# Output projection under the last page's steps, triangular inversion by 64x64 chunks, and the order of the router's last tile, in a hybrid decoder step

## The chip, the cores and the metric

The kernel runs on one core of a Trainium2 chip. The metric is the device time of one execution in microseconds, the median of the runs.

## The reference

One decoder layer for a prompt of 256 tokens and 8 sampled tokens, width 1024, float32, one set of weights for both:

- `p = RMSNorm(h) @ w_in`; its columns feed a gated DeltaNet (4 heads of 128) and a latent attention (4 heads).
- DeltaNet, prompt: exact chunked form, chunk 64. In each chunk and head `lower = tril(k_b k^T * decay, -1)`, `wy = inverse(eye + lower)`, `u = wy @ v_b`, `w = wy @ (k_b exp(g))`, then a scan over the 4 chunks. Sampled tokens: one step of the recurrence on a state of 128x128 a head and token; norm and gate on both.
- Latent attention, sampled tokens: scores against 2048 cached latents each (8 sequences, read through a page table), softmax, sum of latents; prompt: causal.
- `h = h + concat(DeltaNet, latent attention) @ w_out`, where the first 512 rows of `w_out` belong to DeltaNet and the last 512 to the latent attention.
- `h = h + CrossAttention(RMSNorm(h), K and V of RMSNorm(memory))`, then `h = h + MoE(RMSNorm(h))`, top 4 of 32 experts, and a final RMSNorm.

## The kernel before, in words

Every engine has its own instruction list, written out in blocks by hand; semaphores order them, and between blocks all engines meet at a barrier. Three stretches are of interest.

**Inversion (block at L1137).** The 256 prompt tokens are two tiles of 128, so a 128x128 matrix per head and tile `t` holds two chunks of 64 on its diagonal and zeros elsewhere. `X` and its transpose `XT` start from the identity and are doubled in five levels: PE makes `Y = CT·X` (L1203), where `CT` is `LT` masked for the level (L1141, L1148 on DVE); ACT copies `Y` out (L1175); PE makes `XT·Y` and `Y·XT` (L1211, L1212), and DVE subtracts both (L1154, L1155). All four heads of a tile share a PSUM bank. Between the products of a level stands one step each of the sampled tokens' attention, `sampled_pe`, `sampled_act`, `sampled_dve` (`level_steps`): transposes of the cached latents and scores against them. At the end PE makes `u` (L1219) and `wT` (L1220).

**Output projection.** The block at L1306 makes the sampled tokens' recurrence (outer products L1408, state updates L1372), the gated norm (L1362 to L1380) and the last steps, 26 to 35, of the sampled attention. Step 33 takes the last sequence's maximum (L1071), exponent on ACT (L1097), transposes (L1055) and their copy (L1080); step 34 multiplies with the latents (L1061). Then comes a block of its own, `add_projection` (L1503): four tiles of 8 float32 products (L1523) and the sampled rows (L1530), between them the stages of `join_products`, which join the partial softmax sums of the sampled attention, and the transposes of the normed memory (`turn`, L237). `load_cross_weights` on SP reads `x` again into `res` (L1553) when the small sums (L1451) are made, because their operand `acc` lies in that buffer.

**Router's last tile.** The normed rows are split into three bf16 parts: ACT casts (`cast_part`, L2239) and GpSimd takes the cast off the rest (`take_off`, L2349), in turn. For the last tile the residual's second half is joined at L2384 (fifth `joined`), squared on ACT (L2231), scaled (L2390); PE makes the logits, DVE chooses the experts (L2397 to L2402), PE counts positions (L2146), and `gather` (L1957) waits for all parts. A loop over 16 pairs of experts follows (`hidden`, L1974), for which SP streams 402 MB of weights through a ring of 12 buffers; SP refills a buffer when PE has freed it.

## Time and profile before

| | us |
|---|---|
| median of 3 runs | 1519.07 (1518.77 to 1522.3) |
| the profiled execution | 1522.03 |
| its span, first to last instruction | 1520.2 |
| PE busy in the span | 1389.4 |
| DVE busy | 462.6 |
| ACT busy | 240.2 |
| GpSimd busy | 44.6 |

Times in the trace count from the span's start. L12 is line 12 of the kernel before. PE is the TensorE matmul stream, PEld its weight loads, which overlap it; both are recorded per instruction, with modelled ends. A bracket behind a row is the idle time of that engine ahead of it and what ended it.

### The profile page before, as it was taken

The numbers are of one execution on the slowest core, as the hardware profiler recorded it, in microseconds if no ns is written. First come the engines' busy times: TensorE is split into PE (matmuls) and PEld (weight loads), VectorE is DVE, ScalarE is ACT, GpSimd is POOL, SyncE is SP. The second block draws the span as 40 slices with busy tenths as digits, with TensorE's granted clock in tenths as the row PEclk, the third lists the DMA queues.
The fourth block names the chain that finished last, engine by engine and source line by source line (L and its number), as shares of the span: only waits on it lengthen the run. The fifth ranks groups of instructions, "written<-read, shape, count | busy, mean of one in ns | idle before, by whom it ended". The sixth has DMA issues, their size and how long they took to land.

```text
span 1520.2 us, 20735 instructions
## 1 busy us (share of the span) xinstructions
PE 1389.4 (91%) x8299; PEld 696.9 (46%) x8299; DVE 462.6 (30%) x1108; ACT 240.2 (16%) x422; POOL 44.6 (3%) x39
## 2 busy tenths in 40 slices
PE   8999999989999989999999989889889899899896
PEld 6667876645467544333333333333333333333332
DVE  1856543552214242311311311221131122113113
ACT  1143222320002442100100100000001001001002
POOL 0000100000000140000000000000000000000000
PEclk9999999979999999999999999999999999999999
DMA  8120533537463766999999999999999999999996
GB/s 361 38 92 17 195 139 140 188 122 258 160 253 112 250 277 277 426 424 425 427 424 426 426 424 426 425 423 429 424 424 428 424 425 426 424 426 425 424 427 248
DMA packets 96722, 490.66 MB, mean 323 GB/s; under 512 B 9307, under 2 KB 14527, under 8 KB 61626
## 3 DMA queue, kind: packets, MB, share of 16 engines
q1 hardware_dynamic: 94074, 468.89, 75.2%
q0 software_dynamic: 2304, 20.97, 3.6%
q8 instruction: 35, 0.57, 0.2%
q10 hardware_dynamic: 296, 0.11, 0.0%
q14 instruction: 13, 0.11, 0.0%
HBM read 484.01 MB, written 6.04 MB: 322 GB/s over the span
## 4 chain that ended last, share of the span: by engine, by line
PE 39%; DMA 17%; DVE 5%; issue 2%; ACT 1%; POOL 1%; SPq 1%; POOLq 0%; DVEq 0%
DMA arena<-in_w_e 17%; PE ps L1974 15%; PE ps L2010 14%; PE ps L2022 4%; PE ps L1964 1%; PE ps L1997 1%; DVE arena L2540 1%; DVE arena L2550 1%; DVE arena L2547 1%; DVE arena L2548 1%; SPq L1621 1%; PE ps L2038 1%; PE ps L2026 1%; DMA arena<-in_cache_mem_k 1%; POOL arena L2349 1%
## 5 line engine op out<-in xcount | busy, mean ns | idle before, releaser
L1974 PE MATMUL ps<-arena 128*64 128x512 f32 x2048 | 456.2, 595 | 27.6 <-DMA arena<-in_w_e 27.0
L1974 PEld LDWEIGHTS ps<-arena 128*64 128x64 f32 x2048 | 146.2, 137 | 309.6 <-issue 308.2
L2010 PE MATMUL ps<-arena 128*64 128x512 f32 x960 | 217.0, 610 | 2.6 <-ACT arena L2224 2.2
L2010 PEld LDWEIGHTS ps<-arena 128*64 128x64 f32 x960 | 78.1, 142 | 139.0 <-issue 126.1
L2547 DVE TENSOR_SCALAR arena<-ps 128x1024 f32<-128x1024 f32 x15 | 18.4, 1225 | 303.4 <-PE ps L1974 303.4
L2559 DVE COPY arena<-ps 128x512 f32<-128x512 f32 x15 | 10.4, 692 | 219.3 <-PE ps L2010 219.3
L2222 ACT ACTIVATE arena<-arena 128x1024 f32<-128x1024 f32 x15 | 15.9, 1058 | 335.4 <-DVE arena L2547 335.4
L2565 DVE TENSOR_TENSOR res<-res,ps 128x512 f32<-128x512 f32 x60 | 41.2, 687 | 81.2 <-PE ps L2022 81.2
L1997 PE MATMUL ps<-cst,arena 128*128 128x128 f32 x120 | 20.8, 329 | 43.7 <-DVE arena L2540 43.7
L1650 PE MATMUL ps<-arena 128*128 128x512 f32 x128 | 57.5, 608 | 2.1 <-PEq L1507 2.1
L2022 PE MATMUL ps<-arena 128*128 128x512 f32 x120 | 55.5, 605 | 0.0
L1957 PEld LDWEIGHTS ps<-arena 128*128 128x128 bf16 x768 | 49.3, 99 | 13.0 <-issue 12.2
L1957 PE MATMUL ps<-arena 128*128 128x128 bf16 x768 | 53.8, 222 | 0.6 <-ACT arena L2239 0.6
L1089 ACT COPY arena<-ps 128x384 f32<-128x384 f32 x64 | 30.6, 478 | 101.5 <-PE ps L1019 101.5
L2226 ACT COPY arena<-ps 128x512 f32<-128x512 f32 x15 | 8.8, 585 | 220.9 <-PE ps L2010 220.9
L1077 DVE COPY arena<-ps 128x256 f32<-128x256 f32 x64 | 27.1, 423 | 44.0 <-PE ps L1023 40.8
L2531 DVE TENSOR_SCALAR arena<-cst,arena 128x64 bf16<-128x64 f32 (+1 forms) x90 | 22.2, 247 | 58.9 <-PE ps L1991 58.9
L1650 PEld LDWEIGHTS ps<-arena 128*128 128x128 f32 x128 | 24.6, 194 | 32.4 <-issue 32.4
L1997 PEld LDWEIGHTS ps<-cst,arena 128*128 128x128 f32 x120 | 16.4, 168 | 46.4 <-DVE arena L2540 46.4
L2022 PEld LDWEIGHTS ps<-arena 128*128 128x128 f32 x120 | 21.6, 189 | 33.7 <-issue 33.7
L528 PE MATMUL ps<-arena,xnT 128*128 128x392 f32 (+2 forms) x96 | 35.5, 527 | 0.0
L1017 PE MATMUL ps<-cst,arena 128*128 128x128 f32 x128 | 28.4, 305 | 6.7 <-ACT arena L1089 5.1
(551 smaller groups left out, 1571.7 us busy)
## 6 DMA issues: line engine op xcount, KB each, us to landing
arena<-in_w_e SPq DMA_DIRECT2D x384, 1024.0 KB, 18.4
arena<-in_w_in SPq DMA_DIRECT2D x8, 1380.0 KB, 17.6
arena<-in_cache_mem_k SPq DMA_DIRECT2D x8, 1024.0 KB, 8.1
arena<-in_w_out SPq DMA_DIRECT2D x2, 2048.0 KB
arena<-in_w_xk SPq DMA_DIRECT2D x1, 4096.0 KB, 15.0
arena<-in_w_xv SPq DMA_DIRECT2D x1, 4096.0 KB, 12.8
arena<-in_w_xq SPq DMA_DIRECT2D x1, 4096.0 KB, 23.3
arena<-in_cache_mem_v SPq DMA_DIRECT2D x1, 4096.0 KB, 14.8
```

Source lines behind the costliest of these rows:

```text
L528: last = pe.matmul(ps[:, bank, 0:b - a], xnT[:, k, cols(t)], win[:, k, CONV + a:CONV + b], start=(k == 0), stop=(k == KD - 1))
L1017: pe.transpose(ps[:, 5, j * P:(j + 1) * P], lat[:, tile, j * P:(j + 1) * P], ident)
L1077: nc.vector.tensor_copy(KT[:, k % 2, p, 3 * P:5 * P], ps[:, 6, 0:2 * P]).then_inc(sa["odd_moved"], 1)
L1089: nc.scalar.copy(KT[:, k % 2, p, 0:3 * P], ps[:, 5, 0:3 * P]).then_inc(sa["even_moved"], 1)
L1650: last = pe.matmul(ps[:, i % 4, :], memT[:, k, cols(t)], w[:, k, n * 512:(n + 1) * 512], start=(k == 0), stop=(k == KD - 1))
L1957: pe.matmul(out, xp[:, t, i, k * P:(k + 1) * P], picked[:, t, :], start=(t == 0 and i == 0), stop=False)
L1974: last = pe.matmul(ps[64 * x:64 * x + 64, c, :], xe[:, k, 64 * x:64 * x + 64], ring[n % RING][:, c * 512:(c + 1) * 512], start=False, stop ...
L1997: last = pe.transpose(ps[:, 6 + k // 4, (k % 4) * P:(k % 4 + 1) * P], lin[:, k * P:(k + 1) * P], ident)
L2010: last = pe.matmul(ps[64 * x:64 * x + 64, 4 + c, :], aT[:, k, 64 * x:64 * x + 64], ring[(n + x) % RING][:, j * D + c * 512:j * D + (c + 1) ...
L2022: pe.matmul(ps[:, COMBINE_BANKS[2 * t + c], :], gT[:, t, :], ye[:, c * 512:(c + 1) * 512], start=True, stop=True).then_inc(lp["combined"], 1)
L2547: nc.vector.tensor_scalar(glu[:, :].rearrange("p (c n) -> p c n", c=4), hid[:, :, :, 0], 7.0, None, ALU.min).then_inc(lp["glu"], 1)
L2565: nc.vector.tensor_tensor(a, a, ps[:, COMBINE_BANKS[i], :], ALU.add).then_inc(lp["added"], 1)
```

## The change

Three edits.

1. The inversion works on the 64x64 chunks: the chunk of partitions 0 to 63 and that of 64 to 127 lie side by side in memory (`own_blocks`), every product becomes two, each with 64 rows, 64 weight columns and 64 moving columns, and what is copied, masked and subtracted is 256 columns wide. The masks, which sit in different columns for each half, are applied by two instructions.
2. `add_projection` and its block are gone; its work moves to the end of the block before. Half of the first tile (the latent attention's rows of `w_out`) is placed ahead of step 33 on PE, half of the second behind the last outer product; the rest follows the norm's transposes, between the stages of the join. In step 33 DVE takes the maximum ahead of the second norm multiply. Banks of the memory's transposes change from 5 and 6 to 0 and 2. The functions of the join are the same and stand ahead of the block.
3. In the router, ACT squares the last half ahead of the last cast of the sampled rows, DVE takes over the second half of each subtract of the last tile, and GpSimd and DVE write the last part directly as bf16.

```diff
+    def own_blocks(whole):
+        return whole.rearrange("p t h n -> p (t h n)")[:, 0:2 * H * CHUNK].rearrange("p (t h n) -> p t h n", t=2, h=H)
+
+    Xc, CTc, XTc, Yc = (own_blocks(whole) for whole in (X, CT, XT, Y))
+    HALVES = (slice(0, CHUNK), slice(CHUNK, P))
...
-    def level(m):
-        return rep1(c_(C_LVL + m * P), [P, H, P])
+    def level_part(dve, m, t):
+
+        for half in HALVES:
+            mask = cst[half, C_LVL + m * P + half.start:C_LVL + m * P + half.stop]
+            last = nc.vector.tensor_tensor(CTc[half, t], LT[half, t, :, half], rep1(mask, [CHUNK, H, CHUNK]), ALU.mult)
+        return last
 
...
-                nc.vector.tensor_tensor(XT[:, t], rep1(ident, [P, H, P]), CT[:, t], ALU.subtract)
+                link(level_part(dve, 0, t))
+                for half in HALVES:
+                    nc.vector.tensor_tensor(XTc[half, t], rep1(ident[half, half], [CHUNK, H, CHUNK]), CTc[half, t], ALU.subtract)
...
-    def sampled_dve(dve, k):
+    def sampled_dve(dve, k, maximum=True, copies=True):
         b, m = k // 4, k % 4
-        if b > 0 and m == 1:
+        if b > 0 and m == 1 and maximum:
             dve.wait_ge(sa["scored"], 4 * b)
...
+        if not copies:
+            return
...
+    STEP_LAST = 4 * DEC + 1
...
-                        nc.vector.tensor_tensor(X[:, t], X[:, t], ps[:, t, :].rearrange("p (h n) -> p h n", h=H), ALU.subtract)
-                    nc.vector.tensor_tensor(XT[:, t], XT[:, t], ps[:, 2 + t, :].rearrange("p (h n) -> p h n", h=H), ALU.subtract).then_inc(x_ready, 1)
+                        nc.vector.tensor_tensor(Xc[:, t], Xc[:, t], of_heads(t), ALU.subtract)
+                    nc.vector.tensor_tensor(XTc[:, t], XTc[:, t], of_heads(2 + t), ALU.subtract).then_inc(x_ready, 1)
...
-                nc.vector.tensor_copy(wT[:, t], ps[:, 2 + t, :].rearrange("p (h n) -> p h n", h=H))
+            dve.wait_ge(uw_made, 3)
+            for i, half in enumerate(HALVES):
+                nc.vector.tensor_copy(wT.rearrange("p t h n -> p (t h) n")[:, :, half], ps[:, 2 + i, :].rearrange("p (m n) -> p m n", m=2 * H))
...
-                    nc.scalar.copy(Y[:, t], ps[:, t, :].rearrange("p (h n) -> p h n", h=H)).then_inc(y_moved, 1)
+                    nc.scalar.copy(Yc[:, t], ps[:, t, 0:H * CHUNK].rearrange("p (h n) -> p h n", h=H)).then_inc(y_moved, 1)
...
+            def block_of(bank, h, half):
+                return ps[half, bank, h * CHUNK:(h + 1) * CHUNK]
+
             for t in range(2):
                 for h in range(H):
-                    last = pe.transpose(ps[:, 2 + t, h * P:(h + 1) * P], XT[:, t, h, :], ident)
+                    for half in HALVES:
+                        last = pe.matmul(block_of(2 + t, h, half), XTc[half, t, h, :], ident[half, half], start=True, stop=True)
                 last.then_inc(x_turned, 1)
             for m in range(1, LEVELS):
                 for t in range(2):
                     for h in range(H):
-                        last = pe.matmul(ps[:, t, h * P:(h + 1) * P], CT[:, t, h, :], X[:, t, h, :], start=True, stop=True)
+                        for half in HALVES:
+                            last = pe.matmul(block_of(t, h, half), CTc[half, t, h, :], Xc[half, t, h, :], start=True, stop=True)
...
                     for h in range(H):
-                        if m + 1 < LEVELS:
-                            pe.matmul(ps[:, t, h * P:(h + 1) * P], XT[:, t, h, :], Y[:, t, h, :], start=True, stop=True)
-                        last = pe.matmul(ps[:, 2 + t, h * P:(h + 1) * P], Y[:, t, h, :], XT[:, t, h, :], start=True, stop=True)
+                        for half in HALVES:
+                            if m + 1 < LEVELS:
+                                pe.matmul(block_of(t, h, half), XTc[half, t, h, :], Yc[half, t, h, :], start=True, stop=True)
+                            last = pe.matmul(block_of(2 + t, h, half), Yc[half, t, h, :], XTc[half, t, h, :], start=True, stop=True)
...
-                    pe.matmul(ps[:, t, h * P:(h + 1) * P], XT[:, t, h, :], vb[:, t, h, :], start=True, stop=True)
-                    last = pe.matmul(ps[:, 2 + t, h * P:(h + 1) * P], kbe[:, t, h, :], XT[:, t, h, :], start=True, stop=True)
+                    for half in HALVES:
+                        last = pe.matmul(ps[half, t, h * P:(h + 1) * P], XTc[half, t, h, :], vb[half, t, h, :], start=True, stop=True)
                 last.then_inc(uw_made, 1)
+            for t in range(2):
+                for h in range(H):
+                    for i, half in enumerate(HALVES):
+                        place = (t * H + h) * CHUNK
+                        last = pe.matmul(ps[:, 2 + i, place:place + CHUNK], kbe[half, t, h, :], XTc[half, t, h, :], start=True, stop=True)
+            last.then_inc(uw_made, 1)
...
+    mixed = sem("mix_out_made")
+    MIX = ((0, 0, 5), (0, 1, 6), (1, 0, 3), (1, 1, 1))
...
+    memT = Arena(arena, AT_WXO).take([P, KD, MEM])
+    squares, factors, scale, turn, take_out, _ = norm_steps("mem", memt, (0, 1), V_MEM, mem_loaded, 16, AT_WXO + KD * MEM, dst=memT, banks=(0, 2))
...
+            load_cross_weights(sp, n_stored[0])
...
+            join_exps(act)
+            squares(act)
...
                     link(nc.vector.tensor_tensor(sig, sig, z, ALU.mult))
+                    sampled_dve(dve, STEP_LAST, copies=False)
                     link(nc.vector.tensor_tensor(o3, o3, sig.rearrange("p t (h n) -> p (t h) n", n=P), ALU.mult))
                     nc.vector.tensor_scalar(gw[:, 1, :], gw[:, 0, :], 1.0 / P, EPS, ALU.mult, ALU.add).then_inc(gn["var"], 1)
+                    sampled_dve(dve, STEP_LAST, maximum=False)
...
-                    sampled_dve(dve, k)
+                    if k != STEP_LAST:
+                        sampled_dve(dve, k)
...
-                                        vec[:, V_GDN:V_GDN + 1], None, ALU.mult)
+                                        vec[:, V_GDN:V_GDN + 1], None, ALU.mult).then_inc(gn["placed"], 1)
+            join_weights(dve)
+            factors(dve)
+            scale(dve, 0)
+            scale(dve, 1)
+            join_sum(dve)
+            dve.wait_ge(x_loaded, 32)
+            for i, (t, n, bank) in enumerate(MIX):
+                dve.wait_ge(mixed, i + 1)
+                r = res[:, t, n * 512:(n + 1) * 512]
+                nc.vector.tensor_tensor(r, r, ps[:, bank, :], ALU.add)
+                if i == 1:
+                    take_out(dve, 0)
+                    join_out(dve)
+            take_out(dve, 1)
...
         @block.tensor
         def _(pe):
+            def mix_part(i, ks):
+                t, n, bank = MIX[i]
+                for k in ks:
+                    last = pe.matmul(ps[:, bank, :], yT[:, k, cols(t)], wout[:, k, n * 512:(n + 1) * 512],
+                                     start=(k == H), stop=(k == H - 1))
+                    if k == H - 1:
+                        last.then_inc(mixed, 1)
...
+                if h == 3:
+                    mix_part(1, range(H, 2 * H))
                 for k in head_steps(h):
+                    if k == STEP_LAST:
+                        pe.wait_ge(wout_loaded, 32)
+                        mix_part(0, range(H, 2 * H))
                     sampled_pe(pe, k)
             pe.wait_ge(gn["ready"], 1)
...
+            join_products(pe, 0)
+            pe.wait_ge(gn["placed"], 1)
+            mix_part(0, range(H))
+            join_products(pe, 1)
+            mix_part(1, range(H))
+            pe.wait_ge(sa["acc_moved"], DEC)
+            join_products(pe, 2)
+            pe.wait_ge(gn["placed"], NT)
+            turn(pe, 0)
+            mix_part(2, (*range(H, 2 * H), *range(H)))
+            join_products(pe, 3)
+            turn(pe, 1)
+            mix_part(3, (*range(H, 2 * H), *range(H)))
+            pe.wait_ge(jn["y"], 1)
+            for k in range(KD):
+                for j in range(4):
+                    last = pe.matmul(ps[32 * j:32 * j + DEC, 4, 0:D // 4], yT[:, k, cols(2)], wout[:, k, j * D // 4:(j + 1) * D // 4],
+                                     start=(k == 0), stop=(k == KD - 1), tile_position=(0, 32 * j))
+            last.then_inc(mixed, 1)
...
-                tensor(pe, 0)
-                pe.wait_ge(loaded, at)
-                for t in range(2):
-                    for n in range(2):
-                        for k in range(KD):
-                            last = pe.matmul(ps[:, 2 * t + n, :], src[:, k, cols(t)], w[:, k, n * 512:(n + 1) * 512],
-                                             start=(k == 0), stop=(k == KD - 1))
-                        last.then_inc(made, 1)
-                        tensor(pe, 2 * t + n + 1)
-
...
-            pe.wait_ge(mo["parts_ready"], NT)
+            pe.wait_ge(mo["parts_ready"], NT + 1)
...
-            act.wait_ge(mo["left"], 4)
-            cast_part(2, 2).then_inc(mo["parts_ready"], 1)
             act.wait_ge(mo["joined"], 5)
             act_chain.link(act, squares(1, 1))
             act.wait_ge(mo["squared"], 1)
             for half in range(2):
                 act.wait_ge(mo["scaled"], 3 + half)
                 cast_part(1, 0, 512 * half, 512 * (half + 1)).then_inc(mo["part"], 1)
-            for half in range(2):
-                act.wait_ge(mo["left"], 5 + half)
-                cast_part(1, 1, 512 * half, 512 * (half + 1)).then_inc(mo["part"], 1)
-            for half in range(2):
-                act.wait_ge(mo["left"], 7 + half)
-                last = cast_part(1, 2, 512 * half, 512 * (half + 1))
-            last.then_inc(mo["parts_ready"], 1)
+            act.wait_ge(mo["left"], 4)
+            cast_part(2, 2).then_inc(mo["parts_ready"], 1)
+            act.wait_ge(mo["left"], 5)
+            cast_part(1, 1, 0, 512).then_inc(mo["part"], 1)
+            act.wait_ge(mo["left_dve"], 1)
+            cast_part(1, 1, 512, D).then_inc(mo["part"], 1)
...
-            for i in range(2):
-                for half in range(2):
-                    pool.wait_ge(mo["part"], 5 + 2 * i + half)
-                    take_off(1, x_part(1, i), 512 * half, 512 * (half + 1))
+            pool.wait_ge(mo["part"], 5)
+            take_off(1, x_part(1, 0), 0, 512)
+            pool.wait_ge(mo["part"], 7)
+            nc.gpsimd.tensor_tensor(x_part(1, 2)[:, 0:512], left_1[:, 0:512], x_part(1, 1)[:, 0:512], ALU.subtract).then_inc(mo["parts_ready"], 1)
 
         @block.vector
         def _(dve):
...
             join(1, 1, 5)
             dve.wait_ge(mo["pos"], 2)
             link(place_in(2, 7))
+            for i in range(1, XPARTS):
+                last = nc.vector.tensor_copy(slot[32 * i:32 * i + DEC, 2, 0:NE], slot[0:DEC, 2, 0:NE])
+            link(last)
             dve.wait_ge(mo["turned"], 5)
             take_out(1, 1, 3)
             dve.wait_ge(mo["rooted"], 3)
             factor(1)
             for half in range(2):
                 scale(1, 512 * half, 512 * (half + 1))
-            for i in range(1, XPARTS):
-                last = nc.vector.tensor_copy(slot[32 * i:32 * i + DEC, 2, 0:NE], slot[0:DEC, 2, 0:NE])
-            link(last)
-            first_picks(2)
             dve.wait_ge(mo["logits"], 3)
             choose(1, 0)
+            second = slice(512, D)
+            dve.wait_ge(mo["part"], 6)
+            nc.vector.tensor_tensor(left_1[:, second], left_1[:, second], x_part(1, 0)[:, second], ALU.subtract).then_inc(mo["left_dve"], 1)
+            first_picks(2)
             dve.wait_ge(mo["pos"], 3)
             link(place_in(1, 4))
             first_picks(1).then_inc(lp["picked"], 1)
+            dve.wait_ge(mo["part"], 8)
+            nc.vector.tensor_tensor(x_part(1, 2)[:, second], left_1[:, second], x_part(1, 1)[:, second], ALU.subtract).then_inc(mo["parts_ready"], 1)
```

## Rows read from the trace of the kernel before

**Rows 1.** The page, 40 slices of 38 us: busy tenths of the DMA engines.

```profile
DMA  8120533537463766999999999999999999999996
```

**Rows 2.** Windows: stretch, length, busy us (instructions) by engine, granted clock, DMA share, GB/s.

```profile
350.00:354.00 4.00, 4.00 (x33) 3.72 (x34) 0.22 (x1) 0.00 (x0) 0.00 (x0) 0.96 0.21 25
...
565.00:570.00 5.00, 1.07 (x8) 0.94 (x7) 3.86 (x9) 2.98 (x7) 2.60 (x3) 0.53 0.00 0
```

**Rows 3.** Groups of instructions by line and shape, inversion, 152 to 213 us.

```profile
L1212 PE MATMUL ps<-arena 128*128 128x128 f32 x80 | 14.3, 275 | 0.0
...
L1155 DVE TENSOR_TENSOR arena<-arena,ps 128x512 f32<-128x512 f32 x10 | 6.8, 682 | 0.7 <-PE ps L1212 0.7
```

**Rows 4.** Timeline, PE: inversion, scan, first expert; start us, us, instruction, idle before.

```profile
152.02 1.68 PE L1195 MATMUL ps<-cst,arena 128*128 128x128 f32 x8 [2.10 <-PEq L160]
...
202.27 1.95 PE L1212 MATMUL ps<-arena 128*128 128x128 f32 x16
...
234.79 0.43 PE L1277 MATMUL ps<-arena 128*64 128x128 f32 x2
235.15 0.43 PE L1278 MATMUL ps<-arena 64*64 64x128 f32 x2
...
578.77 6.66 PE L1974 MATMUL ps<-arena 128*64 128x512 f32 x30 [0.59 <-DVE arena L2540]
```

**Rows 5.** Timeline, last page's steps and output projection, 312 to 375 us.

```profile
312.50 1.98 PE L1408 MATMUL ps<-arena 8*128 8x512 f32 x4
...
314.41 0.86 PE L1038 MATMUL ps<-arena 128*32 128x128 f32 x24
314.73 1.76 DVE L1367 TENSOR_TENSOR arena<-arena 128x1536 f32<-128x1536 f32 x1
...
318.68 0.68 DVE L1071 TENSOR_REDUCE arena<-ps 128x1 f32<-128x512 f32 x1
...
320.42 1.12 PE L1055 MATMUL ps<-cst,res 128*128 128x128 f32 x4 [5.14 <-ACT res L1097]
...
321.46 3.78 PE L1408 MATMUL ps<-arena 8*128 8x512 f32 x4
...
325.17 3.64 PE L1061 MATMUL ps<-arena,res 128*32 128x256 f32 x32
...
332.69 8.73 PE L1523 MATMUL ps<-arena,xnT 128*128 128x512 f32 x16
...
341.97 7.13 PE L1523 MATMUL ps<-arena,xnT 128*128 128x512 f32 x16
...
348.94 3.63 PE L1451 MATMUL ps<-arena,res 128*128 128x4 f32 x32
...
352.60 0.37 SPq L1553 DMA_DIRECT2D res<-in_x_prompt  x1
...
371.47 3.64 PE L1530 MATMUL ps<-arena,xnT 128*8 128x256 f32 x64
```

**Rows 6.** Timeline, router's last tile until the first gather, 561 to 573 us.

```profile
561.56 0.69 DVE L2384 TENSOR_TENSOR res<-res,ps 128x512 f32<-128x512 f32 x1 [1.91 <-PE ps L2052]
...
563.84 1.04 ACT L2239 CAST arena<-arena 8x1024 bf16<-8x1024 f32 x1 [2.23 <-POOL arena L2349]
...
564.91 0.63 ACT L2231 ACTIVATE arena<-res 128x512 f32<-128x512 f32 x1
...
567.40 4.48 POOL L2349 TENSOR_TENSOR arena<-arena 128x512 f32<-128x512 f32 x4 [3.60 <-ACT arena L2239]
567.50 2.22 DVE L2417 TENSOR_SCALAR arena<-cst,arena 72x64 bf16<-72x64 f32 x2
...
569.64 0.24 DVE L2397 SCALAR_TENSOR_TENSOR arena<-ps,arena 128x32 f32<-128x32 f32 x1
...
570.88 0.64 PE L2146 MATMUL ps<-arena,cst 128*128 128x32 f32 x2 [4.81 <-DVE arena L2401]
...
572.60 0.82 PE L1957 MATMUL ps<-arena 128*128 128x128 bf16 x6 [0.65 <-ACT arena L2239]
```

286 lines of the change are left out of this document (120 added, 166 removed).

## The prediction

> **What bounds the kernel now.** I read the page's forty slices first. From slice 16 on, the DMA engines are full to the end of the span [rows 1]: that is the loop over expert pairs, it streams a fixed amount of weights, and nothing in the change touches it. What the change can do is let that stream start earlier. The windows then show whether it would: in the 5 us ahead of the loop (565 to 570) the DMA moves nothing, PE is busy 1.07 of 5 us and its granted clock is 0.53 [rows 2]. The ring is full by then, and the stream starts again only when PE frees ring buffers with its first hidden products. So before the loop the order of work on PE decides, and a microsecond taken from PE's path there is a microsecond of the whole time, as long as no transfer becomes late. The three edits lie on that path, in three stretches: the inversion (152 to 212 us), the output projection (315 to 375) and the router's last tile (561 to 573). I read each in the timeline, in order of time.
>
> **The inversion.** Every float32 product is two records: 40 products of the line that makes the second half of the last factor are 80 records [rows 3]. Five levels make 40 products C·X, 32 products for X and 40 for XT, so 224 records. Sixteen of them in a row take 1.95 us from the first start to the last end, 0.275 of it the last one's [rows 3, 4], so one starts each (1.95 - 0.275)/15 = 0.111 us. 224 x 0.111 = 24.9 us on PE, which hardly idles there. The change makes each product two of 64 rows by 64 columns by 64 moving columns, on the two diagonal quarters of the array: 448 records, each with half the moving columns and half the weight columns. The trace of before has no two products on different rows of the array side by side, so I bound the spacing. If the quarters take turns, a record costs half of 0.111, 0.0555 us, and 448 of them 24.9 us: nothing is saved. If the quarters run side by side it is half of that again, 0.028 us, and 12.4 us: 12.5 saved. The nearest rows speak for the second: 24 score records on four column strips take 0.86 us, (0.86 - 0.27)/23 = 0.026 each, where one strip alone would need 0.107; and 30 expert records on two strips take 6.66, (6.66 - 0.59)/29 = 0.21 each against 0.43 for the same width on the full array, (7.13 - 0.59)/15 [rows 4, 5]. I take 0.028, because those strips also load different weights beside each other, and keep 0.0555.
>
> The other parts of this stretch cost. The eight single-record transposes ahead of level 1 took 1.68 us at a low clock [rows 4]; they become 32 records, 1.7 us side by side or 3.6 in turns. The products for u and w were 32 records, 3.55 us at 0.111. u becomes 32 records of 128 moving columns: 1.7 side by side, 3.55 in turns. w becomes 32 records with 64 moving columns but still 128 weight columns; where the moving side is only 4 wide, records are still (3.63 - 0.25)/31 = 0.109 us apart [rows 5], so weights bind there, and w costs 1.8 or 3.5. Together 0 saved, or 3.5 lost. Last, changes of shape: in the scan, two records of a 128-row product and two of a 64-row product alternate, and each pair starts 0.36 us after the one before (234.79, 235.15) instead of 0.22 [rows 4], so a change of shape costs 0.14. The transposes of the pages stay 128 wide, so C·X and the second products each get one change before and one behind: 4 a level, 20 in all, 2.8 us.
>
> The vector and scalar engines: evictions stay as many, at 256 columns instead of 512, where a subtract takes 0.68 us now [rows 3]. The masked factors become four instructions of 64 partitions and 256 columns a level instead of two of 128 and 512. By work they cost the same; were each as long as the present subtract, it would be 1.4 us more a level. The 2 us of page transposes and scores that stand between the products of a level hide that; without the cover it would be 5.6 us in all four levels that build a next factor, and I count nothing. Sum of the inversion: 12.5 - 2.8 = **9.7 us saved**; in turns, -2.8 - 3.5 - 1.9 = 8.2 us lost.
>
> Here a rule speaks against the change. The rows show column strips that write the same bank at once. The Trainium skill, TensorEngine Tiling (Array Packing), section Restrictions and Gotchas, says that different row tiles can't access the same PSUM bank at the same time, and both halves of a head write one bank here, though other partitions of it. By that rule the halves would take turns and the sum of this part would be the loss above; no run here shows it yet.
>
> **The output projection.** Before, PE sits idle for 5.14 us in front of the last page's softmax transposes: the maximum starts only at 318.68, behind the second of two 1.76 us multiplies and a state update on DVE, while the scores ended at 315.27 [rows 5]. Behind that gap the same four outer-product records take 3.78 us instead of 1.98 for the head before, and the product with the values 3.64 us: half clock. Then a block boundary, and a first tile of 8.73 us where the second takes 7.13 [rows 5]. The change puts the maximum ahead of the second multiply (the exponent is then done near 317.4), gives PE a half tile (8 records of 0.43 = 3.4 us) in the gap and another behind the fourth outer product, and drops the boundary. From 315.27 the PE path becomes: half tile 3.4; transposes 0.66; outer product 1.98; half tile 3.4; product with the values about 1.9, estimated as half of 3.64; output transposes 1.4; sums transposed 0.3; half tile 3.4; wait for the coefficients and their products 1.1; half tile 3.4; 32 small sums 3.63; turn 0.94; tile 8.73 (the small sums are again followed by a low clock, as the tile behind them was before); value products 1.85; turn 0.94; tile 6.9; sample rows 3.64. That is 47.6 us, to 362.9 (terms under 2 us are read off the same timeline). DVE keeps up: the normalised outputs are ready near 324.3 and the last state update near 326.5, PE needs them at 326.7.
>
> SP issues the same transfers in the same order, and GpSimd's queue issues none here. One transfer gets late: x is read again into the buffer that the small sums free, so it is asked for near 340 instead of 352.6, but now behind the memory tile, one weight and the state store (7.3 MB) that are asked for near 327 and kept the DMA busy until about 350 before; only in the window from 350 to 354 it falls to 0.21 [rows 2]. x then lands near 352, its first sums and the first normed tile on DVE take 2 us more, and the second turn on PE, which needs the banks emptied, waits about 2.5 us. So the sample rows end near 365.4 instead of 375.1 [rows 5]: **9.7 us saved**. Bounds: 12.2 if x isn't late, 6 if the wait also brings a low clock for the last tile and the half tile in the gap runs at half speed. Should the half tiles not be hidden, each costs its 3.4 us, which is the work they take out of the later tiles, so nothing is lost.
>
> **The router's last tile.** The last residual half is added at 561.56, done 562.25. Its squares start at 564.91 only, behind a cast that waited for GpSimd and ran until 564.88; the choice for this tile starts at 569.64, and PE, idle for 4.81 us, goes on at 570.88, 1.24 us later; the gather starts at 572.60, behind the last remainder cast [rows 6]. With squares first, root and factor come about 2.2 us sooner, so the factor is there near 564.0; the two scales behind it on DVE end near 564.9, the time at which I estimate the logits too, so the choice starts at 565.1 and, with nothing in its way, lasts 1.2 us. Its last compare waits for a GpSimd subtract of 1.12 us (four take 4.48), so the choice is done near 566.7. The remainders: ACT casts at 564.5 to 565.7, the moved cast to 566.8, then two more halves to 568.25; GpSimd subtracts one half of each, DVE the other. DVE's second half and its picks overlap with GpSimd's; two picks that took 2.22 us beside GpSimd where 0.42 is their work show what that can cost [rows 6]. Without that cost the last part is ready at 569.2, with it at 570.4: 3.3 or 2.2 us saved. I take **2.7**, between them; PE stays at the low clock there either way, and if it didn't 1.6 more would come.
>
> **Sum.** 9.7 + 9.7 + 2.7 = 22.1 us. The profiled execution took 1522.03 (span 1520.2), so 1499.9 by its own measure; it is 3 us above the median of the runs, 1519.07, which gives **1497**.
>
> **Rivals.** (1) The quarters take turns: -8.2 + 9.7 + 2.7 = 4.2 us, 1515. For it: no row shows row tiles side by side; against: the strips' 0.026 us. That is also the time by the rule above. (2) Transfers hold the projection or the cross-attention back: x and the weights behind it queue in one line, and the saving of the second edit falls to 3 to 5 us: 1503. For it: the DMA is at 1.0 for 20 us there; against: the weights asked for after it are needed 27 us later. (3) Slower: TensorE falls to 1.2 GHz in the inversion. For it: behind the 5.14 us gap the outer products, which use 8 rows of the array, and the value product after them stayed at half clock for 8 us in which PE hardly paused (3.78 and 3.64 us, [rows 5]); the quarters leave half of the array idle too. Against: the scan's 64-row products run at full speed [rows 4]. Each microsecond of PE's work there at half clock costs a second one. From 22 us on the kernel is slower; the stretch would last some 50 us, and 48 of them at half clock would make 1545. (4) The change does little because GpSimd and DVE stall each other and the half tiles aren't hidden: 1506, a piece of case 2's weight.
>
> **Chances.** Forecast 62%, own range 1489 to 1504 (both good ends of the second and third part, and 3 us of shape changes that may not show); turns 20%; late transfers and stalls 11%; low clock 7%. The range must reach the edge of the turns' case to leave out no more than two in ten: 1488 to 1515. Measurements of this kernel can tell about 0.3%, 4.6 us, from no change: forecast, late transfers and a part of the turns' case are faster, 0.82; the rest of the turns' case is no difference, 0.10; low clock and a worse case of turns slower, 0.08.
>
> **What would show it.** Right: second products of a level, 64 records, in about 2 us (32 at 0.111, 3.6, before); the whole stretch 8 to 12 us shorter; no idle in front of the last softmax transposes, projection's sample rows ending 9 to 12 us nearer to the last scores; squares of the last half ahead of the cast and the first gather 2 to 3 us nearer to the residual's add. Wrong: records of 0.055 us in the inversion, a granted clock of 0.5 in it, or PE waiting at the second memory turn for more than 4 us.

## The result, and the profile after

The changed kernel takes 1512.71 us (median of 5 runs, 1508.68 to 1512.73) where the kernel before takes 1522.30 (5 runs, 1518.77 to 1526.12; the 1519.07 of the prediction is the median of the first three): a ratio of 0.9936, 95% interval 0.9922 to 0.9950. That is 9.6 us faster. The forecast was 22 us, 1497. The direction and the range hold, the size doesn't. Of all runs below one stands out, 3553.28 us of bias_loads_later, without a cause that is known; the median given for that kernel is that of its other five.

Cutting both profiled executions at the same points of PE's program gives the account. Times are us; a point is the start of PE's first record of that stage, or the end of its last one, and the last row runs to the end of the span, 1520.2 and 1510.7:

| from, to | before | after | change | forecast |
|---|---|---|---|---|
| start to inversion | 152.02 | 154.14 | +2.1 | 0 |
| inversion to scan | 61.43 | 50.13 | -11.3 | -9.7 |
| scan to the sample's block | 65.52 | 65.52 | 0 | 0 |
| sample's block to the last scores' end | 36.30 | 40.93 | +4.6 | 0 |
| last scores to the memory's first product | 61.91 | 54.66 | -7.3 | -9.7 |
| memory to the second keys' first transpose | 109.83 | 108.88 | -1.0 | 0 |
| these keys, until w_xo's first product | 28.03 | 32.55 | +4.5 | 0 |
| w_xo to the first gather | 57.56 | 55.30 | -2.3 | -2.7 |
| gather to the first hidden product | 6.17 | 7.32 | +1.2 | 0 |
| hidden to the end | 941.43 | 941.27 | -0.2 | 0 |

The three edited stretches give 20.8 us, nearly the forecast. Some 12 us come back in stretches that the diff doesn't touch. For two of them the change need not be the cause: the start of the inversion lies between 152.0 and 154.2 us in the four profiles without the new inversion, and gather to hidden takes 6.2 to 7.4 us in the six without the router's edit. The other two are followed up below: the sample's heads, as the fourth row is called from here on, and the second keys.

The page's slices after (answer to [rows 1]) fill at slice 16 again:

```profile
DMA  9111534348364567999999999999999999999996
```

Groups by line and shape of the inversion after, 154 to 204 us (answer to [rows 3]):

```profile
L1237 PE MATMUL ps<-arena 64*64 64x64 f32 x160 | 9.0, 219 | 0.0
...
L1227 PE MATMUL ps<-arena 64*64 64x64 f32 x160 | 6.9, 240 | 0.2 <-DVE arena L1160 0.2
...
L435 DVE TENSOR_TENSOR arena<-arena,cst 64x256 f32<-64x256 f32 x20 | 8.4, 420 | 4.2 <-PE ps L1227 2.2 <-PEq L160 1.7
```

Timeline of PE after, inversion to the sample's heads (answers to [rows 4]; L1564 are the outer products):

```profile
154.14 1.68 PE L1218 MATMUL ps<-cst,arena 64*64 64x64 f32 x32 [2.10 <-PEq L160]
...
164.47 1.15 PE L1227 MATMUL ps<-arena 64*64 64x64 f32 x32
...
198.73 1.96 PE L1245 MATMUL ps<-arena 64*64 64x128 f32 x32
200.63 2.00 PE L1251 MATMUL ps<-arena 64*128 64x64 f32 x32
204.27 0.41 PE L1028 MATMUL ps<-cst,arena 128*128 128x128 f32 x2 [1.64 <-PEq L1153]
...
277.00 0.38 PE L1028 MATMUL ps<-cst,arena 128*128 128x128 f32 x2 [1.56 <-issue]
...
293.01 1.11 PE L1066 MATMUL ps<-cst,res 128*128 128x128 f32 x4 [0.76 <-ACT res L1110]
```

The 32 records of C·X stand in 1.15 us. At 277.00 PE waits 1.56 us for nothing that the trace shows; behind it, at 293, the softmax transposes take 1.11 us, where 0.60 is what they take below. The granted clock (windows, columns as in [rows 2]) of the sample's heads, before and, in the second row, after; the third row is the projection after:

```profile
278.97:315.27 36.30, 33.57 (x460) 21.10 (x460) 21.55 (x51) 10.90 (x19) 0.00 (x0) 0.86 0.34 125
269.80:310.70 40.90, 37.39 (x461) 23.36 (x461) 21.17 (x50) 10.90 (x19) 0.00 (x0) 0.75 0.30 111
310.70:365.40 54.70, 48.53 (x256) 26.55 (x252) 22.50 (x62) 8.25 (x16) 0.00 (x0) 0.94 0.78 285
```

Timeline of the projection after (answers to [rows 5]):

```profile
310.65 3.70 PE L1539 MATMUL ps<-arena,xnT 128*128 128x512 f32 x8
310.86 0.69 DVE L1082 TENSOR_REDUCE arena<-ps 128x1 f32<-128x512 f32 x1 [0.71 <-PE ps L1049]
...
314.19 0.60 PE L1066 MATMUL ps<-cst,res 128*128 128x128 f32 x4
314.72 1.98 PE L1564 MATMUL ps<-arena 8*128 8x512 f32 x4
...
335.22 6.99 SPq L1418 DMA_DIRECT2D res<-in_x_prompt  x1
...
347.54 1.28 DVE L1523 TENSOR_TENSOR res<-res,ps 128x512 f32<-128x512 f32 x2 [12.09 <-DMA res<-in_x_sample]
349.57 1.94 PE L237 MATMUL ps<-cst,arena 128*128 128x128 f32 x8 [3.22 <-DVE arena L245]
...
351.30 7.62 PE L1539 MATMUL ps<-arena,xnT 128*128 128x512 f32 x16
...
358.86 3.64 PE L1596 MATMUL ps<-arena,xnT 128*8 128x256 f32 x64
```

The 5.14 us gap in front of the transposes is gone, and the outer products behind it are at full speed. DVE then stands 12.09 us at x, and PE 3.22 us at the second turn behind it. Then the second key pages of the cross-attention, after and (second fence) before:

```profile
474.26 3.00 PE L2049 MATMUL ps<-cst,arena 128*128 128x128 f32 x24 [1.46 <-PEq L160]
...
478.92 15.66 SPq L1918 DMA_DIRECT2D arena<-in_cache_mem_k  x4
...
484.74 1.09 PE L2049 MATMUL ps<-cst,arena 128*128 128x128 f32 x8
...
490.31 1.97 PE L2049 MATMUL ps<-cst,arena 128*128 128x128 f32 x8 [4.48 <-DMA arena<-in_cache_mem_k]
492.21 1.94 PE L2057 MATMUL ps<-arena 128*32 128x256 f32 x16
```

```profile
487.01 4.38 PE L2038 MATMUL ps<-cst,arena 128*128 128x128 f32 x24 [2.42 <-PEq L160]
...
500.96 1.09 PE L2038 MATMUL ps<-cst,arena 128*128 128x128 f32 x8 [1.53 <-DMA arena<-in_cache_mem_k]
501.98 1.07 PE L2046 MATMUL ps<-arena 128*32 128x256 f32 x16
```

After 4.48 us of idle the next transposes and scores run at half speed (1.97 and 1.94 us for 1.09 and 1.07). The wait grew from 1.53 us for two reasons. Counted from the block's first transposes, PE stands at these pages after 11.57 us instead of 12.42, mainly because the first 24 transposes take 3.00 us instead of 4.38; and the first page is there after 16.05 us instead of 13.95. So 0.9 us come from a faster PE and 2.1 us from a later page. The loads in front of the page are the same in both kernels; why they took longer isn't shown.

Last, the router's tile after, until the first gather (answer to [rows 6]), and one row of the same copies before:

```profile
553.33 0.69 DVE L2392 TENSOR_TENSOR res<-res,ps 128x512 f32<-128x512 f32 x1 [1.91 <-PE ps L2063]
...
554.05 0.63 ACT L2242 ACTIVATE arena<-res 128x512 f32<-128x512 f32 x1 [0.67 <-DVE res L2392]
554.14 1.66 DVE L2509 COPY arena<-arena 8x32 f32<-8x32 f32 x2
...
556.59 1.30 PE L2074 MATMUL ps<-arena 128*128 128x32 f32 x8 [1.85 <-DVE arena L2395]
...
562.11 0.82 PE L1968 MATMUL ps<-arena 128*128 128x128 bf16 x6 [1.66 <-DVE arena L2527]
```

```profile
567.11 0.36 DVE L2507 COPY arena<-arena 8x32 f32<-8x32 f32 x2
```

The squares start 0.03 us behind the residual's add, as forecast, and the gather stands 8.1 us behind that add's end (562.11 - 554.02) instead of 10.35 (572.60 - 562.25, [rows 6]). But the two slot copies, moved ahead of the last turned tile, run beside a GpSimd subtract and take 1.66 us instead of 0.36.

### The profile page after: what moved, and what is told of

Same layout as the page of the kernel before. It is cut to its first block, busy times and chain, and to the rows that moved or that the text cites. A ratio compares the mean times of both kernels' runs of the same rounds, so it can differ in the third digit from the quotient of the medians.

```text
span 1510.7 us, 21293 instructions
## 1 busy us (share of the span) xinstructions
PE 1395.6 (92%) x8579; PEld 692.9 (46%) x8579; DVE 461.6 (31%) x1124; ACT 237.4 (16%) x420; POOL 42.5 (3%) x37
## 4 chain that ended last, share of the span: by engine, by line
PE 41%; DMA 17%; DVE 6%; issue 2%; ACT 1%; SPq 1%; POOL 1%; DVEq 0%
DMA arena<-in_w_e 16%; PE ps L1985 15%; PE ps L2021 15%; PE ps L2033 4%; PE ps L1975 2%; PE ps L2008 1%; DVE arena L2553 1%; DVE arena L2563 1%; DVE arena L2560 1%; DVE arena L2561 1%; DMA arena<-in_cache_mem_k 1%; PE ps L2063 1%; PE ps L2049 1%; SPq L1632 1%; PE ps L2037 1%
## 5 line engine op out<-in xcount | busy, mean ns | idle before, releaser
L1985 PE MATMUL ps<-arena 128*64 128x512 f32 x2048 | 454.5, 595 | 17.8 <-DMA arena<-in_w_e 17.2
L2021 PE MATMUL ps<-arena 128*64 128x512 f32 x960 | 227.5, 634 | 2.2 <-ACT arena L2235 2.0
L1968 PEld LDWEIGHTS ps<-arena 128*128 128x128 bf16 x768 | 50.3, 100 | 14.0 <-issue 12.2
## 6 DMA issues: line engine op xcount, KB each, us to landing
arena<-in_w_in SPq DMA_DIRECT2D x8, 1380.0 KB, 17.7
```

The source lines that it names most:

```text
L1968: pe.matmul(out, xp[:, t, i, k * P:(k + 1) * P], picked[:, t, :], start=(t == 0 and i == 0), stop=False)
L1985: last = pe.matmul(ps[64 * x:64 * x + 64, c, :], xe[:, k, 64 * x:64 * x + 64], ring[n % RING][:, c * 512:(c + 1) * 512], start=False, stop ...
L2021: last = pe.matmul(ps[64 * x:64 * x + 64, 4 + c, :], aT[:, k, 64 * x:64 * x + 64], ring[(n + x) % RING][:, j * D + c * 512:j * D + (c + 1) ...
```

## The experiments

All times are medians; ratios are to the kernel before, run on the same chip, with their 95% interval. The kernels ran on several chips, on which the kernel before takes 1521.1 to 1522.3 us, and a ratio's interval is 2 to 4 us to either side: a difference between two kernels' medians is no surer than that. Differences between stretches of two traces are given beside them.

**Each part alone.** Three kernels hold one of the three edits, a fourth moves the key pages in the changed kernel.

> The kernel before with the inversion by 64x64 chunks alone. Theory A (a microsecond taken from TensorE's path ahead of the loop is a microsecond of the whole): the trace of the changed kernel took 11.3 us out of the inversion, so the whole is 9 to 11 us shorter than before. Theory B (part is given back further on, in the sample's heads and at the cached memory keys): the scan starts 9 to 11 us earlier, but the last scores end only 4 to 6 us earlier, and the whole is 4 to 6 us shorter.

Measured 1520.06 us, ratio 0.9988 (0.9975 to 1.0000), while its one profiled execution, 1514.09, was the fastest of twelve. In it the inversion took 50.15 us, 11.3 less, and the last scores ended 10.1 us earlier. Theory A falls; the 2.2 us of the whole are less than B's 4 to 6, too, and can't be told from none.

> The kernel before with the output projection's order alone (inversion and router as before). Theory A: last scores to sample rows 8 to 9.7 us shorter and the whole 8 to 9.7 us shorter. Theory B: the stretch is 7 to 8 us shorter, 2 to 4 us of it come back as a longer wait for the cached memory keys and a lower clock behind it, and the whole is 4 to 6 us shorter.

Measured 1518.59, 0.9976 (0.9964 to 0.9988): 3.7 us, so A falls and B's 4 to 6 are just missed. In the trace the stretch from the last scores to the memory is 5.4 us shorter, memory to keys 2.7, and the keys take 2.2 us more, with a wait of 2.9 us.

> The kernel before with the router's last tile alone. Theory A: last residual sum to first gather 2.2 to 3.3 us shorter and the whole as much. Theory B (the gather then runs behind an idle TensorE at the lower clock): the whole is 1 to 1.5 us shorter.

Measured 1520.60, 0.9988 (0.9976 to 1.0001); w_xo to gather 55.28 us, 2.3 less. The whole is 1.7 us shorter, and its interval holds both A's 2.2 to 3.3 and B's 1 to 1.5. Together the three parts give 7.5 us against their chip's 1522.26. Theory A fails for the inversion and the projection; for the router it stays open.

**The keys.** The diff of keys_first (later kernels that name keys hold it too):

```
-            fill(sp, 3, 0)
-            sp.wait_ge(stored, memory_stored)
-            for i in range(3):
-                sp.dma_start(bias..., b_e1[0]) ; sp.dma_start(bias..., b_e2[0])
             for b in range(G):
                 sp.wait_ge(sx["scored"], b + 1)
                 sp.dma_start(Kx[:, b], cache_mem_k[0, G + b]...)
+            (the five lines above, here)
```

> The changed kernel with the second four cached key pages asked for ahead of the loop's fourth weight tile and the six bias loads. Theory B: the pages wait behind those loads; TensorE's wait of 4.5 us for the first of them falls under 1 us and the transposes behind it keep the full clock, so the whole is 3 to 5 us shorter than the changed kernel (1508 to 1510 us). Theory A has no such loss: unchanged within 0.3% (1510 to 1515 us).

Measured 1505.87, 0.9886 (0.9867 to 0.9904): 6.8 us under the changed kernel, more than expected. No transpose of the keys waits for a page, the step takes 25.3 us instead of 32.6, all of it at full clock.

> The kernel before (nothing of the change) with the second four key pages asked for ahead of the fourth weight tile and the bias loads. In the changed kernel this step took 6.8 us off. Theory B (the change brings TensorE to the keys before their transfer, and loses there what it saved): before has only 1.5 us of wait there, so the step gives it 1 to 3 us (1519 to 1521 us), and change plus step against before plus step is 13 us or more. Rival C (the step is worth the same with or without the change, and the keys took nothing from it): 5 to 7 us (1515 to 1517 us).

Measured 1520.50, 0.9990 (0.9976 to 1.0003): 1.4 us, theory B; C falls. Without the change PE's wait was 1.53 us. So most of what the keys cost came with the change: change and step against step alone are 14.6 us. B's reason holds for the smaller part only, since of the longer wait 0.9 us are PE's earlier arrival and 2.1 the page's later one.

> The changed kernel with only the six bias loads behind the second key pages; the loop's fourth weight tile (1 MB) stays ahead of them. Theory B1 (the bias loads, during which the queues moved only 162 to 281 GB/s, hold the pages up): wait for the first page under 1 us, time as keys_first, 1505 to 1507 us. Theory B2 (the weight tile holds them up): wait and time as in the changed kernel, 1511 to 1513 us.

Measured 1504.30 (five runs), 0.9894 (0.9871 to 0.9917), and no wait for the pages: B1, 0.7 us under its 1505 to 1507. It is the six small loads, not the weight tile. Nor is it SP, whose wait for earlier stores moved together with the loads: the first page is asked for 4.7 us behind the weight tile in both kernels (474.21 and 478.92 in the changed one, 472.06 and 476.76 here). While the small loads run, the changed kernel's DMA engines are busy throughout and move about half of the 425 GB/s of the loop, or less (last two columns: DMA share, GB/s):

```profile
480.00:482.00 2.00, 2.00 (x25) 1.26 (x24) 1.31 (x2) 1.10 (x2) 0.00 (x0) 1.00 0.96 162
482.00:484.00 2.00, 2.00 (x24) 1.73 (x26) 0.92 (x2) 0.82 (x2) 0.00 (x0) 1.00 1.00 213
484.00:486.00 2.00, 1.83 (x24) 1.12 (x16) 0.59 (x2) 0.49 (x2) 0.00 (x0) 1.00 1.02 223
```

The Trainium skill, DMA: Bandwidth & Descriptors, section Queues, rings and completion order, says that each DMA engine takes up the descriptors of an issuer's ring in their order, though a later one may finish its write first; the trace agrees with the first part, since putting the pages ahead of six loads of the same issuer ends a 4.5 us wait.

**The turn.** In turn_first_alone, and with the keys in keys_turn_first:

```
+            take_out(dve, 0)
             dve.wait_ge(x_loaded, 32)
             for i, (t, n, bank) in enumerate(MIX):
                 ...
                 if i == 1:
-                    take_out(dve, 0)
                     join_out(dve)
```

> keys_first with VectorE taking the memory's first turned tile out of PSUM ahead of its wait for x. Theory B: TensorE's 3.2 us of idle ahead of the second turn go, last scores to the first product of the memory falls from 54.5 us to 51 to 52 us, and the whole is 2 to 3.2 us shorter than keys_first (1502.7 to 1504 us). Theory E (the weights behind it set the time): last scores to memory is shorter, but the whole stays within 1 us of keys_first.

Measured 1499.03, 0.9852 (0.9830 to 0.9874), 6.8 us under keys_first for an idle of 3.13 us there, more than B's 2 to 3.2, so E falls. Of this the two traces show 6.3 us, 4.6 up to the memory's first product and 1.7 from there to the keys. The rows show why: the turn and the tile behind it (1.94 and 7.62 us in the changed kernel) are at full speed again.

```profile
346.50 1.07 PE L237 MATMUL ps<-cst,arena 128*128 128x128 f32 x8
347.41 7.03 PE L1539 MATMUL ps<-arena,xnT 128*128 128x512 f32 x16
354.38 3.64 PE L1596 MATMUL ps<-arena,xnT 128*8 128x256 f32 x64
```

So is the memory's first product behind the block's boundary: 7.11 us for 16 records, 8.80 in keys_first. Last scores to memory fell from 54.5 to 49.9 us, memory to keys from 108.9 to 107.2.

> The changed kernel with only VectorE's order changed: the memory's first turned tile is taken out of PSUM ahead of the wait for x (the keys as in the changed kernel). On top of keys_first this took 6.8 us. Theory B (TensorE's wait for the second key pages is counted from their own block's start, so what is saved ahead of it stays saved): last scores to the memory's first product 50 us in place of 54.7, the keys' wait again 3 to 5 us, the whole 5 to 7 us under the changed kernel (1506 to 1508 us). Rival G (the pages land at a fixed time, so an earlier TensorE waits the longer): the wait grows to 8 us or more and the whole stays at 1511 to 1513 us.

Measured 1507.81, 0.9907 (0.9886 to 0.9928), 4.9 us under the changed kernel, with the keys' wait as long as ever though PE came 8 us earlier:

```profile
482.86 1.97 PE L2049 MATMUL ps<-cst,arena 128*128 128x128 f32 x8 [4.88 <-DMA arena<-in_cache_mem_k]
```

G falls: the page came 7.5 us earlier as well (482.86 against 490.31), so the wait doesn't eat what was saved ahead of it. The whole's 4.9 us lie just under B's 5 to 7.

**The wait for nothing.** All nine profiled executions with the new inversion and w_out at its old place show PE waiting 1.6 to 1.9 us in one of the steps behind the block's 128 short products; the four without the new inversion show none, though there, too, w_out's loads fall on these products. keys_w_out_late:

```
-            for half in range(2):
-                load_w_out(sp, half)
             store(sp, gdn_prompt[0, 0]..., S[:, :, :])
+            sp.wait_ge(sm["outer"], 1)
+            for half in range(2):
+                load_w_out(sp, half)
```

> keys_first with w_out's 4 MB asked for behind the first outer product instead of at the sample block's start. Theory B: the 1.6 to 1.9 us in which TensorE waits for nothing visible, 7 us into that block, are a fetch of instructions that stands behind w_out's packets; it falls under 0.4 us, the stretch from the sample block's start to the last scores' end falls from 39.4 us to 36 to 38 us, and the whole is 1.5 to 3.5 us shorter than keys_first. Rival D (the fetch is slow by itself after 128 short matmuls): the wait stays at 1.6 us or more and the time is that of keys_first.

The wait is gone; the 128 products and the steps behind them follow without a pause:

```profile
270.26 3.67 PE L1554 MATMUL ps<-arena 128*8 128x128 f32 x127
273.86 0.44 PE L1028 MATMUL ps<-cst,arena 128*128 128x128 f32 x2
...
274.56 0.86 PE L1049 MATMUL ps<-arena 128*32 128x128 f32 x24
275.35 0.44 PE L1028 MATMUL ps<-cst,arena 128*128 128x128 f32 x2
```

So D falls as a mechanism: the wait needs w_out's packets beside it, and something that only the kernels with the new inversion have. That it is a fetch of instructions fits: of the instruction queue, q8, one packet lands among w_out's on q1 between 274 and 275 in the changed kernel.

```profile
q1 hardware_dynamic: 97, 0.40, 98.2%
q8 instruction: 1, 0.02, 5.8%
```

Such a packet starts 4.9 to 5.3 us behind the block's first record in all 13 profiles with w_out at its old place, and after 2.1 us in the three with w_out late. But the 13 hold the four in which PE doesn't wait, and the trace doesn't say for which engine the packet came, so this stays inferred.

Nor did taking the wait away make the stretch shorter. The stretch is 37.5 us as expected, but it is 37.4 us with the wait in inversion_only and turn_first_alone, whose scans took 65.5 us like the one here; where the scan took 67.0 to 67.1, the stretch is 38.8 to 39.4 us with the wait and 39.1 without (copies_behind). Where the idle went, the lower clock lasted longer: granted 0.86 in inversion_only, 0.82 here, with 3.8 and 2.6 us of idle.

```profile
267.80:305.19 37.39, 33.63 (x460) 20.68 (x460) 21.57 (x51) 11.02 (x19) 0.00 (x0) 0.86 0.34 121
269.76:307.28 37.52, 34.88 (x461) 21.94 (x461) 21.17 (x50) 10.91 (x19) 0.00 (x0) 0.82 0.33 121
```

The whole, 1505.07, 0.9896 (0.9873 to 0.9918), can't be told from keys_first; its six times fall into two groups, 1501.2 to 1502.9 and 1507.2 to 1508.9.

> keys_turn_first with w_out asked for behind the first outer product as well. Theory B: no wait for instructions in the sample block, sample block's start to last scores' end 36.3 to 37.6 us in place of 39.3, the whole 1.5 to 3 us under keys_turn_first (1496 to 1497.5 us). Rival D (as keys_w_out_late's median hints, whose times went from 1501 to 1509 us): w_out's later packets cost elsewhere what the wait gave, and the time is 1498 to 1500 us.

Measured 1494.97, 0.9840 (0.9814 to 0.9865): the fastest median here, 17.7 us under the changed kernel, with 37.5 us in the sample's heads. Its interval overlaps that of keys_turn_first, its five times fall into two groups as well (1493.9 to 1495.0, 1499.4 and 1500.3), and its profile has the shorter scan (65.5 us against 67.1), so the last step's own worth stays unsettled.

**The inversion's worth.**

> inversion_only with the key pages first, to be set against before_keys_first (1520.5 us), in which nothing of the change is. Theory A (all that the inversion saves stays saved once the keys are out of the way): 9.7 to 11.3 us, so 1509 to 1511 us. Theory B (1.9 us go to TensorE's wait for instructions in the sample block and 1 to 4 us to the lower clock in scan and sample heads): 5 to 8 us, so 1512.5 to 1515.5 us.

Measured 1515.78, 0.9952 (0.9935 to 0.9970): 4.7 us against before_keys_first, 0.3 us beyond the poor end of B; by the two ratios it is 5.8 us, inside B. The trace has -11.0 in the inversion, +1.6 in the scan, +3.0 in the sample's heads and +2.3 ahead of the inversion.

> A second profile of inversion_only, whose first was 6 us under its own median. Theory B: the inversion is 50 to 52 us again, and the loss lies in the sample's heads (37.4 us from the block's start to the last scores' end then, 36.3 us before): 39 to 43 us. Rival F (the inversion itself runs at the lower clock in other executions): the inversion takes 54 us or more, the sample's stretch 37 to 38 us.

The inversion took 50.7 us, the sample's heads 38.8, a little under B's 39; the scan took 67.0 instead of 65.5, and F falls for this kernel. In keys_first, changed_again and copies_behind, though, the inversion took 51.9 to 52.0 us, at a granted clock of 0.93 instead of 0.97. One run, 1518.96.

> A second profile of the changed kernel itself. Theory B (the wait for instructions and the wait for the key pages belong to the change, the long stretch at the lower clock in the sample's heads and the 2 us later start of the inversion to the single execution): 1.5 to 1.9 us and 4 to 5 us of these waits again; the sample's heads 37.4 to 39.4 us where the first profile had 40.9. Theory A' (all of it belongs to the change): 40.5 us or more again.

Theory B, but for the keys: 1.8 us for nothing, 5.3 us at the keys (B had 4 to 5), 39.3 us in the heads, so 1.6 of the first profile's 40.9 were that execution's. The scan took 67.1, and the inversion began at 155.45. One run, 1516.06, above all five of the first set, on a chip on which the kernel before took 1521.14: the 9.6 us of the result rest on five runs on one chip.

**The copies.**

```
-            for i in range(1, XPARTS):  last = nc.vector.tensor_copy(slot[32 * i...], slot[0:DEC...])
-            link(last)
             dve.wait_ge(mo["turned"], 5)
             take_out(1, 1, 3)
+            (the removed lines, here)
```

> keys_turn_w_out with VectorE's two small slot copies behind the last turned tile's take-out instead of ahead of it. In the changed kernel these copies took 1.66 us beside GpSimd's subtract (0.36 us where they stood before), and TensorE waited 1.85 us for the take-out behind them. Theory B: the take-out comes 1 us sooner, that wait falls to 0.9 us or less and the first gather comes 0.5 to 1.3 us nearer to the residual's last add (8.07 us there): whole 0.5 to 1.3 us shorter, about 1494 us. Rival H (the last remainder, which waits for ScalarE's casts, sets the gather): the wait is shorter, the gather as far behind the add as before, whole the same within 0.4 us.

The copies took 0.36 us again, PE's wait for the take-out fell from 1.85 to 0.85 us (another one of 0.90, for a compare on DVE, came behind it), and the gather came 0.5 us nearer to the add, the lower end of B. The whole, 1497.00, 0.9838 (0.9817 to 0.9859), is no shorter than keys_turn_w_out; 0.5 us is less than these runs can tell. The profiled execution is even 8.0 us longer than the one of keys_turn_w_out, all of it ahead of the last scores, where the two kernels don't differ. The trace speaks against H, the time decides nothing.

## Why the prediction was right in its terms and wrong in its sum

**The step that failed** is the first: "a microsecond taken from PE's path there is a microsecond of the whole time, as long as no transfer becomes late". One part of it held: from the first hidden product to the end every profile here has 941.2 to 941.5 us, so an earlier start is an earlier end. But I summed the three edited stretches and took all that lies between as fixed; they gave 20.8 us, and the whole 9.6. The condition, late transfers, was checked for x and the weights, not for each wait on PE's way to the loop. Two losses stand in its place.

- The second key pages. Their 1.53 us wait stood in the trace of before. With the change it is 4.5 to 5.3 us in the three profiles with the router's and the projection's edits and the keys unmoved: PE comes 0.9 us sooner, counted from that block's first transposes, and the page 2.1 to 2.9 us later, behind the six bias loads. Moving the page ahead of them gave 6.8 us. Why the loads took longer than before stays open.
- The sample's heads, 36.3 us in all four profiles without the new inversion, 40.9 in the first profile of the change and 39.3 in the second. With the new inversion either PE idles longer there (3.8 us in inversion_only against 2.7 before, at the same 0.86) or the clock is lower (0.82 in keys_w_out_late, with 2.6 us of idle), or both. No run gave this back, and its cause stays open.

**Inversion**, forecast 9.7: 11.3 in the stretch. The spacing taken, 0.028, is there: (1.15 - 0.24)/31 = 0.029 us. The 64 records of a level's second products take 2.1 us (159.81 to 161.87 in the first level), as said. u and w take 3.9 us for 3.84 before, nothing, as said. Of 12.5 for the products 11.3 are left; so 1.2 us, not 2.8, remain for changes of shape and all else, a remainder that no run measured by itself. The mask parts, 0.42 us each, hide behind the pages' steps. The rule that I weighed against this (the Trainium skill, TensorEngine Tiling (Array Packing), Restrictions and Gotchas) doesn't hold in the form in which I applied it: both quarters wrote one bank, on other partitions, at 0.029 us a record, where turns would give 0.055. The products for u say the same: they kept their 128 moving columns and write one bank with both halves, and yet start (1.96 - 0.27)/31 = 0.055 us apart instead of 0.111. Rival 1 falls. But the whole got 4.7 us of it (inversion_keys_first). Of the 11.0 us in that trace 3.0 come back in the sample's heads, 1.6 in the scan at the lower clock (67.0 to 67.1 us in seven of twelve profiles with the new inversion, 65.5 in the other five and in all four without) and 2.3 ahead of the inversion, where the change does nothing. The wait for nothing stands in the heads, but the heads were as long without it. Why the scan meets the lower clock in some executions stays open, as do the up to 3.7 us by which the inversion's start varies (152.0 to 155.7); router_only and projection_only, which change nothing ahead of it, have 154.2 and 153.7.

**Projection**, forecast 9.7 with 2.5 us of waiting for x, bounds 6 to 12.2: last scores to the sample rows' end fell from 59.8 to 51.8 us, 8.1. The mechanism was right at each step: no gap, x late, the wait at the second turn. Counted from the last scores' end, x landed where I said (after 36.8 us, forecast 36.7) and PE was there nearly as said (35.6, forecast 36.1). But it waited 3.22 us, not 2.5, and at a price that I had put into the lower bound only: the clock behind it made the turn 0.9 us and the tile 0.6 us longer than in keys_turn_first. With that wait taken away the same stretch is 47.0 us, 12.85 saved. In projection_only, where it was 6.2 us shorter, the whole kept 3.7, with the keys' wait against it.

**Router**, forecast 2.7 between 2.2 and 3.3: 2.3 here, 1.8 to 2.3 in the other profiles with the router's edit as it is. My sum has no term for the two slot copies: 0.36 us at their old place, 1.66 beside a subtract of GpSimd, and moving them back brought the gather 0.5 us nearer. I had priced that effect for the picks and not for them. Counted on to the first hidden product the edit is worth a little less: w_xo to there takes 62.3 to 62.8 us in the ten profiles with it and 63.7 to 65.0 in the six without.

**Rivals.** Late transfers (2) is the nearest to what came true, at the keys as well as at x, and its 1503 was still too low: it has no low clock behind the waits and nothing for the sample's heads. Low clock in the inversion (3) falls, it ran at 0.97 before and after. Stalls between GpSimd and DVE (4) are the 1.3 us of the copies, of which 0.5 reached the gather. keys_turn_first, with two waits out of the way and no edit to PE's program, takes 1499.03 against a forecast of 1497, but that is in part luck. Its trace has 17.4 us less than before from the last scores to w_xo's first product, where I had forecast 9.7 (those two edits also take away what the keys' wait had cost before, 1.4 us in before_keys_first), and 4.6 us more in the scan and the sample's heads, where I had forecast none.

## What to carry to other kernels

A stretch made shorter is worth its microseconds only if nothing on the way to the next bound starts to wait: list every wait of the bounding engine from the edit to that bound, the short ones too, and ask from what its arrival is counted. Price an idle on TensorE with the half-speed work behind it: taking 3.1 us of idle at the second turn away gave 6.3 us in the traces. But look at the trace again afterwards: taking 1.85 us of idle away in the sample's heads gave nothing, because the lower clock lasted longer. Put what TensorE needs next ahead of small loads in the same queue, and take banks out ahead of a wait for a load that they don't need.

## What the hardware did that I had not expected

Six loads of biases (1.2 MB in all by their shapes) kept the DMA engines busy at 162 to 223 GB/s, so that 1 MB behind them had PE waiting until 11.4 us after its issue; with the page ahead of them it landed 4.8 us after its issue (keys_first). SP's own issue of x took 6.99 us behind 7.3 MB that it had asked for 12 to 13 us earlier, where it took 0.37 [rows 5]. In the kernels with the new inversion PE paused 1.6 to 1.9 us for nothing visible when w_out's 4 MB fell on 128 short products, and not when they were asked for 13.6 us later; in those with the old one it never did. An 8x32 copy on DVE went from 0.18 to 0.83 us beside a GpSimd subtract.
